# Key indices for four heads at a time, with two of the large products made on GpSimd

## The reference, cut to what matters

```python
q = (xb @ w_q).reshape(tb, PEER_HEADS, 2, PEER_HALF)            # 8 heads, two halves of 128
sc = jnp.einsum('thjd,hjnd->thjn', q, sub_keys)                 # 128 scores for each half
s_half, i_half = lax.top_k(sc, K)                               # K = 16
cand = (s_half[:, :, 0, :, None] + s_half[:, :, 1, None, :]).reshape(tb, PEER_HEADS, K * K)
cand_idx = (i_half[:, :, 0, :, None] * N_KEYS + i_half[:, :, 1, None, :]).reshape(...)
top_s, top_pos = lax.top_k(cand, K)
idx = jnp.take_along_axis(cand_idx, top_pos, axis=-1)           # 128 of 16384 experts for a token
g = jax.nn.softmax(top_s, axis=-1)
h = jax.nn.gelu(jnp.einsum('td,thkd->thk', xb, u[idx]), approximate=False)
out = jnp.einsum('thk,thkd->td', g * h, v[idx])
```

## Time and profile before

| what | value |
|---|---|
| three runs, us | 1459.85, 1461.23, 1462.47; median 1461.23 |
| the profiled execution, us | 1465.86 |
| its span in the trace, us | 1464.1 |
| mean granted TensorE clock | 0.989 of full speed |
| busy: PE, DVE, POOL, ACT | 1384.9, 1124.6, 621.6, 392.5 us |
| bytes moved | 466.65 MB, mean 319 GB/s |

### The profile page before, as it was taken

The page is one execution under the profiler, slowest core; times in us unless marked ns, Lnnn a source line. Parts: engine busy times, 40 slices in busy tenths (PEclk is TensorE's granted clock), DMA queues, the critical chain, the costliest instruction groups (busy, mean ns, idle before and its releaser), DMA issues.

```text
span 1464.1 us, 16370 instructions
## 1 busy us (share of the span) xinstructions
PE 1384.9 (95%) x5430; PEld 941.3 (64%) x5430; DVE 1124.6 (77%) x2672; ACT 392.5 (27%) x1073; POOL 621.6 (42%) x516
## 2 busy tenths in 40 slices
PE   7999999997989999999999989999999999999994
PEld 5656647555478888878899879985444444444441
DVE  3445445699889999989999889997777767775667
ACT  3323332334221112012377667672000000000000
POOL 0000000331735542342466656666376755654541
PEclk9999999999999999999999999999999999999997
DMA  6423334773999998798799999999999999999997
GB/s 215 149 90 121 115 136 159 274 280 130 383 364 377 373 331 295 251 381 288 245 387 392 368 366 377 382 380 376 400 374 409 409 410 409 409 410 409 409 409 309
DMA packets 140084, 466.65 MB, mean 319 GB/s; under 512 B 14560, under 2 KB 14944, under 8 KB 139232
## 3 DMA queue, kind: packets, MB, share of 16 engines
q0 software_dynamic: 73728, 268.47, 47.8%
q1 hardware_dynamic: 66272, 197.14, 35.8%
HBM read 461.36 MB, written 4.19 MB: 318 GB/s over the span
## 4 chain that ended last, share of the span: by engine, by line
DVE 33%; DMA 28%; PE 24%; issue 9%; POOL 5%; ACT 1%; SPq 0%; another core or an unknown queue 0%; DVEq 0%; ACTq 0%; POOLq 0%
PE BANKS L597 10%; DMA UV<-v,IDX 9%; DVE X L1371 8%; DMA BIG<-v,IDX 7%; DMA BIG<-u,IDX 6%; PE BANKS L591 6%; DMA UV<-u,IDX 5%; PE BANKS L811 4%; POOL UV L1416 4%; DVE UV L1366 2%; DVE BIG L1366 2%; POOL BIG L1416 2%; DVE BIG L1205 2%; DVE BIG L1197 2%; DVE BIG L1199 1%
## 5 line engine op out<-in xcount | busy, mean ns | idle before, releaser
L1416 POOL DMA_INDIRECT UV<-u,IDX x154 | 186.7, 1212 | 385.7 <-DVE IDX L1256 262.8
L1416 POOL DMA_INDIRECT UV<-v,IDX x156 | 198.6, 1273 | 179.9 <-DVE UV L1366 107.1
L786 PE MATMUL BANKS<-T 128*128 128x256 f32 x1024 | 233.1, 383 | 3.5 <-issue 2.7
L1371 DVE SCALAR_TENSOR_TENSOR X<-UV,HG,X 128x1024 f32<-128x1024 f32 x156 | 200.3, 1284 | 44.8 <-DMA UV<-v,IDX 40.6
L786 PE MATMUL BANKS<-T,Y 128*128 128x256 f32 x1024 | 229.7, 380 | 0.1
L811 PE MATMUL BANKS<-T,BIG 128*128 128x512 f32 x512 | 225.4, 593 | 1.5 <-DVE BIG L1387 1.5
L811 PE MATMUL BANKS<-Y,BIG 128*128 128x512 f32 x512 | 225.1, 592 | 0.0
L1366 DVE SCALAR_TENSOR_TENSOR UV<-UV,Y 128x1024 f32<-128x1024 f32 x154 | 187.0, 1223 | 42.7 <-DMA UV<-u,IDX 41.0
L786 PEld LDWEIGHTS BANKS<-T 128*128 128x128 f32 x1024 | 193.7, 192 | 30.7 <-issue 4.5
L786 PEld LDWEIGHTS BANKS<-T,Y 128*128 128x128 f32 x1024 | 192.6, 191 | 25.5 <-DMA Y<-u_t 0.5
L1416 POOL DMA_INDIRECT BIG<-u,IDX x102 | 120.3, 1180 | 154.6 <-DVE X L1371 50.6
(11 more groups left out here) (255 smaller groups left out, 1204.4 us busy)
## 6 DMA issues: line engine op xcount, KB each, us to landing
T<-u_t SPq DMA_DIRECT2D x64, 512.0 KB
Y<-u_t SPq DMA_DIRECT2D x64, 512.0 KB
T<-v SPq DMA_DIRECT2D x64, 512.0 KB
Y<-v SPq DMA_DIRECT2D x64, 512.0 KB
BIG<-w_in SPq DMA_DIRECT2D x24, 1024.0 KB, 7.3
BIG<-w_q SPq DMA_DIRECT2D x16, 1024.0 KB, 7.9
BIG<-w_out SPq DMA_DIRECT2D x8, 1024.0 KB, 6.1
UV<-v,IDX POOLq DMA_INDIRECT x156
```

Source lines behind the costliest of these rows:

```text
L786: last = nc.tensor.matmul(PS[i % 4][:, 0:HT], ub[:, c, :], T8[:, 1, c, :], start=(c == 0), stop=(c == KC - 1))
L1371: stt(xb, row, HG[:, n % 2, i % UNIT:i % UNIT + 1], xb, ALU.mult, ALU.add).then_inc(used, 1)
L1416: pool.indirect_dma_start(row_place(s), None, u if kind == "ru" else v, bass.IndirectOffsetOnAxis(IDX[:, b, c:c + 1], 0)).then_inc(row_in[ ...
```

## The change

Keys of the streamed blocks are now made for four heads at once, over 1024 elements in place of 512, in three steps: `ya` (small operations and the first compare), `yb` (first sum and second compare) and `y` (second sum). The two products between them are done by GpSimd, which waits for the semaphore `oh_compared` and raises `oh_weighed`. Six rows stand between `ya` and `yb` and six between `yb` and `y`. The large operand lies in block 3 of Y, which was the stream's fourth buffer; the stream has three now. The first of the four quarters of the scores that are set aside is no longer taken along, so `away` is 768 KB. The pacing of the first 64 tiles is 3.44 us for each tile with a start of 8 us less. Units 0 to 7 keep the old function.

```diff
-    cost = {"r": 6.2, "y": 5.0, "ru": 1.31, "rv": 1.29, ...}
+    cost = {"r": 4.9, "ya": 2.7, "yb": 2.5, "y": 1.3, "ru": 1.22, "rv": 1.25, ...}
-    for n in (8, 9, 10, 11, 12, 13, 14, 15, 4):
-        first, second, keys = pick(n)
-        work += [first] + rows(3) + (on("oh", 0) if n == 4 else []) + [second] + rows(3) + [keys] + rows(2 + n % 2)
+    for n in (9, 11, 13, 15):
+        for q, item in enumerate(many("r", 4 * (n // 2), 4 * (n // 2) + 4)):
+            work += [item] + rows(2)
...
+        work += on("ya", n) + rows(6) + on("yb", n) + rows(6) + on("y", n)
...
+    first, second, keys = pick(4)
+    work += [first] + rows(4) + on("oh", 0) + [second] + rows(3) + [keys] + rows(1) + on("ws", 3)
...
-        while w < len(work) and spent < 4.1 * (j + 1):
+        while w < len(work) and spent < 3.44 * (j + 1) - 8:
...
-                  Y[:, HB, :], Y[:, HB + 1, :]]
+                  Y[:, HB, :]]
...
-                    sp.dma_start(away, SCA1.rearrange("p a n -> p (a n)")).then_inc(sc_away, 16)
+                    sp.dma_start(away, SCA1[:, 1:4, :].rearrange("p a n -> p (a n)")).then_inc(sc_away, 16)
...
+                    tt(oh, bc(PABF[:, 0, :], 2, TOPK), bc(COLS[:, V_FIRST:V_FIRST + TOPK], 1, nh * TOPK), ALU.is_ge)\
+                        .then_inc(oh_compared, 1)
+                elif step == "yb":
+                    dve.wait_ge(oh_weighed, done + 1)
+                    nc.vector.tensor_copy(PABF[:, 1, :], PAB[:, 4, :])
+                    link(nc.vector.reduce_sum(isel[:, 0, :], oh, AXX))
+                    tt(oh, bc(IOTA[:, 0:TOPK], 1, nh * TOPK), bc(PABF[:, 1, :], 2, TOPK), ALU.is_equal)\
+                        .then_inc(oh_compared, 1)
+                else:
+                    dve.wait_ge(oh_weighed, done + 2)
+                    link(nc.vector.reduce_sum(isel[:, 1, :], oh, AXX))
...
-            for s in range(len(ROWSEQ)):
+            for step, i in ORDER:
+                if step not in ("ya", "yb"):
+                    continue
+                while PLACES[s][2] is None or PLACES[s][2] < rows_until((step, i)):
+                    fetch(s)
+                    s += 1
...
+                pool.wait_ge(oh_compared, n + 1)
+                nc.gpsimd.tensor_tensor(o4, o4, bc(STEP[:, :, :] if step == "ya" else TOPIF[:, :, 1, :], 2, TOPK),
+                                        ALU.mult).then_inc(oh_weighed, 1)
```

More of the change, by code:

```diff
@@ L377, in block_program @@
         COPIED = {g: n for n, g in enumerate(g for g in range(NGRP) if JS[g] < NKEY)}
-        late = lambda n: int(n >= LATE and n < NUNIT)
-        CHOSEN = nth(("r",))
+        kind_of = lambda n: 2 if n >= NUNIT else int(n >= LATE)
+        CHOSEN, FOURS = nth(("r",)), nth(("ya",))
         EXPS = nth(("e",))
@@ L519, in _ @@
                 if j < NS:
-                    sp.wait_ge(hd_full, NKEY - NS + j + 1)
+                    sp.wait_ge(hd_full, NKEY - (NKEY - 1 - j) % NS)
                 else:
@@ L1209, in choose @@
                 n = b * (PH // 2) + h // 2
-                _, CAND, _, TOPS, _, _, POS, TOPI, _, _ = pick_space(late(n))
-                if late(n):
+                _, CAND, _, TOPS, _, _, POS, TOPI, _, _ = pick_space(kind_of(n))
+                if kind_of(n) == 1:
                     dve.wait_ge(sc_back, 16)
@@ L1215, in choose @@
                 dve.wait_ge(ks_done, b // 2 * 8 + h // 2 * 2 + b % 2 + 1)
-                sc = (SC_BACK if late(n) else SC[b]).rearrange("p a (i n) -> p (a i) n", n=NKEY)
-                top16([(sc[:, 2 * h + j, :], TOPV[:, j, :], TOPI[:, h % 2, j, :]) for j in range(2)])\
+                sc = (SC_BACK if kind_of(n) == 1 else SC[b]).rearrange("p a (i n) -> p (a i) n", n=NKEY)
+                top16([(sc[:, 2 * h + j, :], TOPV[:, j, :], TOPI[:, h % POS.shape[1], j, :]) for j in range(2)])\
                     .then_inc(chosen, 1)
@@ L1257, in keys_of_choice, with keys_of_four @@
                         ALU.mult, ALU.add).then_inc(idx_ready, 1)
+            def keys_of_four(step, n):
+                b, q = n // 4, n % 4
+                OH, _, _, TOPS, TOPIF, PABF, POS, TOPI, PAB, STEP = pick_space(kind_of(n))
+                nh = POS.shape[1]
+                to = slice((q + 1) * UNIT - nh * TOPK, (q + 1) * UNIT)
+                isel = ISELS[:, b - HB, :, to]
+                oh = OH.rearrange("p (k c) -> p k c", c=TOPK)
+                o4 = OH.rearrange("p (h k c) -> p h k c", h=nh, c=TOPK)
+                done = 2 * FOURS[("ya", n)]
+                if step == "ya":
+                    g = G[:, b, to].rearrange("p (h k) -> p h k", k=TOPK)
+                    last = tt(g, TOPS[:, :, :], TOPS[:, :, 0:1].broadcast_to([P, nh, TOPK]), ALU.subtract)
+                    if n in RAW:
+                        last.then_inc(g_raw, 1)
+                    pos = POS[:, :, :].rearrange("p h k -> p (h k)")
+                    for m, (first, _, c) in enumerate(COVER[1:]):
+                        ts(PAB[:, m, :], pos, FIRST_OF[first], c, ALU.is_lt, ALU.mult)
+                    nc.vector.tensor_copy(PABF[:, 0, :], pos)
+                    nc.vector.tensor_copy(STEP[:, :, 0:1], TOPI[:, :, 0, 0:1])
+                    link(nc.vector.tensor_copy(TOPIF[:, :, :, :], TOPI[:, :, :, :]))
+                    tt(STEP[:, :, 1:TOPK], TOPIF[:, :, 0, 1:TOPK], TOPIF[:, :, 0, 0:TOPK - 1], ALU.subtract)
+                    tt(PAB[:, 0, :], PAB[:, 0, :], PAB[:, 1, :], ALU.bitwise_or)
+                    link(ts(PAB[:, 2, :], PAB[:, 2, :], 1, None, ALU.bitwise_or))
+                    dve.wait_ge(ks_done, 16)
+                    link(tt(PAB[:, 3, :], PAB[:, 0, :], PAB[:, 2, :], ALU.bitwise_or))
+                    tt(PAB[:, 4, :], pos, PAB[:, 3, :], ALU.bitwise_and)
+                    tt(oh, bc(PABF[:, 0, :], 2, TOPK), bc(COLS[:, V_FIRST:V_FIRST + TOPK], 1, nh * TOPK), ALU.is_ge)\
[9 more added lines that the diff above has]
+                    link(nc.vector.reduce_sum(isel[:, 1, :], oh, AXX))
@@ L1352, in _ @@
                     choose(i // PH, i % PH)
+                elif step in ("ya", "yb") or step == "y" and i >= NUNIT:
+                    keys_of_four(step, i)
                 elif step == "y":
@@ L1453 @@
     args.append(nc.dram_tensor("out", (SEQ, DM), F32, kind="ExternalOutput").ap())
-    args += [nc.dram_tensor(k, (P, 4 * HALF), F32, kind="Internal").ap() for k in ("away", "x_kept")]
+    args += [nc.dram_tensor(k, (P, n * HALF), F32, kind="Internal").ap() for k, n in (("away", 3), ("x_kept", 4))]
     block_program(nc, *args)
```

64 lines of the change are left out of this document (38 added, 26 removed).

## The result

| | kernel before | changed kernel |
|---|---|---|
| median of the runs, us | 1460.54 (4 runs, 1455.20 to 1462.47) | 1482.55 (4 runs, 1481.17 to 1484.57) |
| the profiled execution, us | 1465.86 | 1481.17 |
| its span, us | 1464.1 | 1479.3 |

The ratio is 1.0158 with a 95% interval of 1.0128 to 1.0188: the changed kernel is 1.6% slower. I had forecast 1463.0 and a range up to 1473.

The account below looks back on a forecast made before the run. VectorE's rows were taken to end the kernel, 14.0 us after TensorE. Tail -14.0, later second one-hot +10.8 and three buffers +5.0 made +1.8 us on the median 1461.23: 1463.0 us, range 1447 to 1473.

Parts of the forecast that it names:

- Three buffers: First 64 tiles and start of the `v` stream: tiles asked for 6.9 us ahead, not 10.3; +5 us, ends 0 and 12.
- the rival: `v` stream: tiles landing later than 6.9 us stop TensorE; 0.1 us a tile, 12 us, 1475; chance 0.17 with long holds.
- The sign that I had given for it: Weight loads that wait all through the last stretch would show three buffers to be too few.
- GpSimd's products: Before the second one-hot: each of eight products holds a VectorE row 2.0 us (0 to 4.0), 16 us in all.
- VectorE's own list: Before the second one-hot: four-head keys save 19.3 us, 12 more rows cost 14.1, so 5.2 us shorter.
- My sum of 10.8: Second one-hot, and TensorE with it, 10.8 us later: 16 us of holds less 5.2 of shorter VectorE list.
- The twelve rows: Rows leaving the tail: worth at least 16.7 us, 13.7 after 3 off; gain capped at -14.0 us by TensorE's end.
- The pace: First 64 tiles: late rows make TensorE wait for ScalarE's places in BIG; adds nothing, small chance inside the other cases.
- The sum: Whole kernel: -14.0 + 10.8 + 5.0 = +1.8 us, put on the median 1461.23 to give 1463.0.

Follow-up runs that it names:

- e1: Changed kernel with its fourth stream buffer (block 3 of Y) back and the large operand in block 3 of X: 1459.35 us, ratio 0.9989 to the kernel before.
- e4: Changed kernel with four stream buffers and the products back on VectorE: 1454.47 us, ratio 0.9963.
- e2: Kernel before with three stream buffers in place of four, nothing else changed: 1478.97 us, ratio 1.0129.
- e5: e1 with VectorE choices of the next group, then two rows, beside six of the eight GpSimd products: 1453.65 us, ratio 0.9943.
- e8: e4 without the 12 rows moved ahead of the second one-hot: 1451.66 us, ratio 0.9916.
- e9: e5 with each GpSimd product put ahead of fetches not needed yet: 1451.28 us, ratio 0.9935.
- e7: e1 with each GpSimd product over two of its four heads, 512 elements in place of 1024: 1449.53 us, ratio 0.9911.
- e6: e1 with each GpSimd product replaced by a memset of the same 1024 elements, which reads nothing: 1443.45 us, ratio 0.9869.

## Why the prediction was wrong, and where it was right

**The step that failed is "Three buffers".** It had +5 us, with ends of 0 and 12. Measured, it is 23.2 us (four buffers put back into the changed kernel), with 18.8 us in the kernel before, where part is hidden. Even the 5 us that it had were partly luck: the tile behind `away` waited 2.76 us where I had said 1 to 3, but the one behind `x_kept`, for which I had said about 4, was late by 0.56 us at its weight load, and the other wait, 3.09 us, is of a tile that I had not named. What was missing above all is the other tiles: I had taken a tile's landing as half of a transfer twice its size, 5.4 us of the earlier trace rows, and concluded that 6.9 us are enough. The landing is 6.8 us: the time doesn't halve with the size while the row fetches fill the DMA engines. The list of DMA issues of the kernel before gives no landing time for single tiles, but the earlier trace rows does: the tile behind `away` was asked for at 1010.78 and released its weight load at 1017.50, 6.7 us later, and the tile behind `x_kept` took from 1021.23 to 1031.41. 6.7 us leave next to nothing of 6.9; I had these rows, and took the half of another transfer. I had also put "after 1031 no weight load waited" against the rival. That row shows four buffers, with a margin of 10.3 us; it says nothing of three. The rival named the mechanism and the point from which it decides, and shared a chance of 0.17 with longer holds; its price of 0.1 us a tile was 0.2 us in the run, 3.65 less 3.45. The sign that I had given for it came true, weight loads that wait as long as the row fetches run. Its own 1475 us lay outside my range already.

**GpSimd's products** were right in the mechanism, a row that waits for the product. I had 2.0 us for each of eight, 16 us; it was 2.15 and 17.2. That the size came so near is luck: my 2.0 was the longest fetch, a wait and its own work, and says nothing of how long a product is. The row, not the product alone, shows it: no VectorE row beside a fetch was ever long, and one beside a product is 3.37 us. The Trainium skill (SBUF — State Buffer, Who interferes with whom) says that two inputs in SBUF on VectorE contend with a GpSimd instruction that reads, not with one that only writes, and that the second to start blocks; the rows agree on all three points: held by the product (3.37 us), not by the memset (1300 ns at most), and the product itself waits about 1 us for the row that was there first.

**VectorE's own list.** Forecast 5.2 us shorter without the products; holds of 17.2 less 5.2 would make 12.0, and between the kernel before with three buffers and e1 the ledger shows 12.0. My sum of 10.8 was 1.2 short, by the size of the hold. The changed kernel waits 10.57 us where I had asked for 10 or more, but as e4 showed the wait isn't the measure: the moment itself moved from 720.64 to 728.46, 7.8 us.

**The twelve rows.** With four buffers (e1) the rows ended at 1449.2, 8.4 us sooner than before, although the second one-hot came 7.6 us later: they bought about 16.0 us, where I had 13.7 to 16.7. With three buffers they ended at 1436.0, 13 us sooner still. A stream that asks for a tile each 3.65 us in place of 3.45 leaves the row fetches more of the DMA engines; that is my reading, and the kernel before with one buffer less (e2) fits it: its rows, unchanged, end at 1447.3 in place of 1457.6. The gain is capped by TensorE as I had written. For e1 the two steps together, -14.0 + 10.8, put `fin` at 1457.7 - 3.2 = 1454.5, and it started at 1453.37. Its median was 0.8 us below that of before, within what can be told from no change, and not 3.2; the profiled execution of before was a long one.

**The pace** played no part: nothing in the stage of `u_t` waits for ScalarE's places. The margin of 6.9 us that I gave the tiles of `u_t` was not one either: they land in 6.4 to 6.6 us, and TensorE waited for eight of them, 5.2 us in all, up to 1.1 us at a time. But the wait for the second one-hot covers this (728.46 with three buffers, 728.27 with four).

**The sum as it came out:** -0.8 (the change with four buffers, by medians) + 23.2 (the buffer) = +22.4, against the 22.0 us between the medians of 1482.55 and 1460.54. The median of e1 stands in both terms, so the sum has to come out; what it shows is the split: without the lost buffer the change is worth nothing that can be told from zero, where I had -3.2.

## What to carry to other kernels

Before a buffer is taken from a stream, read the landing time of its own transfers in the stretch where the queues are full, add the issue, and compare with the time that remains; a ring of three tiles whose turn is 0.6 us too long loses 0.2 us at every tile, here 128 times, while the absence of waits says nothing of how much margin there is. A product moved to GpSimd held VectorE's rows, which read two operands, and not its choices, which read one; its place in GpSimd's list counts too, since VectorE waited 5.8 us for one that stood behind ten fetches. Time given to or taken from the list ahead of a meeting point moves both what ends the kernel and what runs up to it, so an edit is to be priced at both ends; the four versions with four buffers that remove holds (e4, e5, e8, e9) gave 1451.3 to 1454.5 us, ratios of 0.992 to 0.996.

## What the runs showed of the hardware

- A product of 128x1024 fp32 on GpSimd takes 2.35 to 2.37 us by itself (the twelve of e5 and e9 that stand beside choices), and makes one two-operand row on VectorE 3.37 us where it is 1.22. At 128x512 the hold is 1.07. In the changed kernel, e1 and e7 eight products held eight rows, never two for one product: the row that meets it waits to its end.
- The choices (`MAX8`, `FIND_INDEX8`, `MATCH_REPLACE8`, one large operand each) run at their usual speed beside a product: 4.8 us for a choice. A GpSimd memset of 128x1024 takes 0.95 us, and no row beside the eight of e6 was held (1300 ns at most).
- A transfer of 512 KB lands 6.8 us after its issue while the row fetches run, with three buffers and with four; 1024 KB took 10.7 and 11.0 us before, 10.4 in the changed kernel, 9.8 in e1 and 12.3 and 11.9 in e2. Twice the size cost 1.4 to 1.8 times the time, not 2.
- With three buffers the lateness doesn't grow: the 99 waits of weight loads are 0.7 us on the mean, none over 2.0 us after the one at 1023. The stream settles at 3.65 us a tile; each wait delays the next request as well, which is my reading of why it doesn't grow.
